# Gate and up chunks: high and low parts of four pairs of plain weight groups made by one instruction per pair

## The reference

```python
def swiglu(x, w_gate, w_up, w_down):
    return (jax.nn.silu(x @ w_gate) * (x @ w_up)) @ w_down

h = h + 0.5 * swiglu(rms_norm(h, ffn1_norm[l]), ffn1_w_gate[l], ffn1_w_up[l], ffn1_w_down[l])
... # mixing block
h = h + 0.5 * swiglu(rms_norm(h, ffn2_norm[l]), ffn2_w_gate[l], ffn2_w_up[l], ffn2_w_down[l])
```

## Time and profile before

| | |
|---|---|
| median of 3 runs | 1835.87 us |
| profiled execution | 1837.03 us |
| its span on the core | 1834.9 us |
| PE busy | 1817.6 us, 99% of the span |
| DVE busy | 1504.9 us, 82% |
| ACT busy | 997.4 us, 54% |
| HBM traffic | 207 GB/s over the span |
| TensorE's granted clock | 0.999 of full speed |

### The profile page before, as it was taken

One profiled execution on the slowest core, in us unless ns is written; L12 is line 12 of the kernel. 1 busy time (PEld: TensorE's weight loads), 2 busy tenths in 40 slices (PEclk: granted clock), 3 DMA queues, 4 the chain that ended last, 5 costly groups with the idle time before them and its releaser, 6 DMA issues.

```text
span 1834.9 us, 29704 instructions
## 1 busy us (share of the span) xinstructions
PE 1817.6 (99%) x10674; PEld 1544.7 (84%) x10674; DVE 1504.9 (82%) x1754; ACT 997.4 (54%) x1181; POOL 11.1 (1%) x23
## 2 busy tenths in 40 slices
PE   8999999999999999999999999999999999999998
PEld 7888888888888888999998878888888888888886
DVE  5888888888998986688966866688888888899996
ACT  7455555555555655754535665545555555555554
POOL 1000000000000000000000000000000000000000
PEclk9999999999999999999999999999999999999999
DMA  7767776777766778565433558577767677676664
GB/s 239 230 212 222 231 221 206 227 218 233 241 199 210 220 227 266 176 185 143 139 111 108 175 171 264 178 229 234 230 220 233 216 226 225 218 237 199 208 216 149
DMA packets 207850, 380.35 MB, mean 207 GB/s; under 512 B 16016, under 2 KB 35728, under 8 KB 207504
## 3 DMA queue, kind: packets, MB, share of 16 engines
q1 hardware_dynamic: 206768, 377.08, 65.3%
q10 hardware_dynamic: 480, 1.97, 0.3%
q0 software_dynamic: 512, 0.06, 0.0%
HBM read 360.19 MB, written 18.87 MB: 207 GB/s over the span
## 4 chain that ended last, share of the span: by engine, by line
PE 92%; DVE 3%; DMA 2%; ACT 1%; issue 1%; SPq 0%; ACTq 0%; DVEq 0%
PE psA L427 30%; PE psB L427 28%; PE psB L1231 6%; PE psT L438 5%; PE psM L438 5%; PE psA L438 5%; PE psA L1231 4%; PE psB L438 2%; PE psM L427 1%; DVE wlo L410 1%; DMA raw<-in_w_in 1%; PE psA L1242 1%; PE psB L650 1%; DMA raw<-in_ffn_w_down 0%; DVE y L1455 0%
## 5 line engine op out<-in xcount | busy, mean ns | idle before, releaser
L401 ACT CAST whi<-raw 128x1024 fp32r<-128x1024 f32 (+1 forms) x648 | 676.6, 1049 | 693.6 <-DVE raw L1455 186.1
L410 DVE TENSOR_TENSOR wlo<-raw,whi 128x1024 fp32r<-128x1024 f32 (+1 forms) x648 | 771.8, 1214 | 205.2 <-ACT whi L401 192.4
L427 PE MATMUL psA<-whi,xh 128*128 128x512 f32 (+1 forms) x576 | 221.8, 385 | 0.5 <-DVE wlo L410 0.5
L427 PE MATMUL psA<-whi,xl 128*128 128x512 f32 (+1 forms) x576 | 221.2, 384 | 0.0
L427 PE MATMUL psA<-wlo,xh 128*128 128x512 f32 (+1 forms) x576 | 221.2, 384 | 0.0
L427 PE MATMUL psB<-whi,xh 128*128 128x512 f32 x544 | 211.7, 389 | 0.0
L427 PE MATMUL psB<-whi,xl 128*128 128x512 f32 x544 | 211.6, 389 | 0.0
L427 PE MATMUL psB<-wlo,xh 128*128 128x512 f32 x544 | 211.6, 389 | 0.0
L427 PEld LDWEIGHTS psA<-whi,xh 128*128 128x128 f32 x576 | 108.4, 188 | 22.0 <-DVE wlo L410 0.7
L427 PEld LDWEIGHTS psA<-whi,xl 128*128 128x128 f32 x576 | 108.4, 188 | 21.3
L427 PEld LDWEIGHTS psA<-wlo,xh 128*128 128x128 f32 x576 | 108.4, 188 | 21.1
(11 more groups left out here) (511 smaller groups left out, 3436.7 us busy)
## 6 DMA issues: line engine op xcount, KB each, us to landing
raw<-in_ffn_w_gate SPq DMA_DIRECT2D x176, 512.0 KB, 4.5
raw<-in_ffn_w_up SPq DMA_DIRECT2D x176, 512.0 KB, 4.6
raw<-in_ffn_w_down SPq DMA_DIRECT2D x176, 512.0 KB, 4.5
raw<-in_w_in SPq DMA_DIRECT2D x80, 512.0 KB, 3.7
raw<-in_w_out SPq DMA_DIRECT2D x32, 512.0 KB, 4.3
quads_dram<-stage SPq DMA_DIRECT2D x88, 128.0 KB, 4.3
stage<-quads_dram SPq DMA_DIRECT2D x22, 512.0 KB, 4.3
x<-in_x SPq DMA_DIRECT2D x4, 512.0 KB, 7.6
```

Source lines behind the costliest of these rows:

```text
L401: nc.scalar.copy(whi[:, slot, :, 0:ncol], raw[:, slot, :, 0:ncol]).then_inc(hi_ready, 1)
L410: nc.vector.tensor_tensor(wlo[:, slot, :, 0:ncol], raw[:, slot, :, 0:ncol], whi[:, slot, :, 0:ncol].bitcast(F32), ALU.subtract).then_inc(l ...
L427: mm = nc.tensor.matmul(ps[:, tb, 0:ncol], lhs[:, k0 + t, tok], rhs[:, slot, t, 0:ncol], start=(first and t == 0 and p == 0 and tb != open ...
```

## The change

In the 20 passes of `chunk(n)`, four pairs of neighbouring plain groups, (0, 1), (2, 3), (6, 7) and (12, 13), are split by one ACT copy and one DVE subtraction of 2048 elements per partition each. The pairs stand in slots that lie side by side (0 and 1, or 2 and 3). The copy waits for both DMAs and for PE to have finished group g - 3, the second one's forerunner in its slot; each instruction counts its semaphore up by 2 at its end. Groups 4, 5, 8 to 11, 14 and 15, the first chunks, the down projections and the mixing block stay as they are, and so do PE's and SP's instructions and their waits.

```diff
--- before.py
+++ after.py
@@ -47,6 +47,7 @@
 CHUNK = ([("gate", j) for j in (0, 1, 4, 5)] + [("unit", 0)] + [("gate", j) for j in (6, 7)] + [("up", 0)] + [("unit", 1)]
          + [("up", j) for j in (1, 4, 5, 6, 7)])
 UNITS = ((7, 7), (7, 8))
+TWO_GROUPS = (0, 2, 6, 12)
 GATE_TOTAL = GATE_UNITS * (FC - 1)
 GATE_STEPS = 5 * (FC - 1)
 PAIR_STEPS = 7
@@ -410,6 +411,22 @@
             nc.vector.tensor_tensor(wlo[:, slot, :, 0:ncol], raw[:, slot, :, 0:ncol],
                                     whi[:, slot, :, 0:ncol].bitcast(F32), ALU.subtract).then_inc(lo_ready, 1)
 
+        def split_hi_two(base, n, per, j):
+            g = base + j
+            two = slice(g % SLOTS, g % SLOTS + 2)
+            wait_raw(nc.scalar, g, n, per)
+            wait_raw(nc.scalar, g + 1, n, per)
+            nc.scalar.wait_ge(group_used, n * per + g - SLOTS + 2)
+            nc.scalar.copy(whi[:, two, :, :], raw[:, two, :, :]).then_inc(hi_ready, 2)
+
+        def split_lo_two(base, n, per, j):
+            g = base + j
+            two = slice(g % SLOTS, g % SLOTS + 2)
+            nc.vector.wait_ge(hi_ready, n * per + g + 2)
+            nc.vector.wait_ge(group_used, n * per + g - SLOTS + 2)
+            nc.vector.tensor_tensor(wlo[:, two, :, :], raw[:, two, :, :],
+                                    whi[:, two, :, :].bitcast(F32), ALU.subtract).then_inc(lo_ready, 2)
+
         def wait_group(base, n, per, j):
 
             nc.tensor.wait_ge(lo_ready, n * per + base + j + 1)
@@ -732,7 +749,10 @@
 
             def chunk(n):
                 for kind, j, g in chunk_items():
-                    split_hi(base, n, PER, g)
+                    if g in TWO_GROUPS:
+                        split_hi_two(base, n, PER, g)
+                    elif g - 1 not in TWO_GROUPS:
+                        split_hi(base, n, PER, g)
                     if kind == "unit":
                         unit = FIRST_UNIT[f] - GATE_UNITS + j
                         nc.scalar.wait_ge(col_step, n * (4 * GATE_UNITS) + (4 * unit + 2))
@@ -958,7 +978,9 @@
                         unit_lo(n, unit)
                         if j == 0:
                             turn_quads(n - 1)
-                    else:
+                    elif g in TWO_GROUPS:
+                        split_lo_two(base, n, PER, g)
+                    elif g - 1 not in TWO_GROUPS:
                         split_lo(base, n, PER, g)
                     if g == 1 and not (isinstance(n, int) and n == 1):
                         turned_lo(n - 2)
```

## The result

The changed kernel takes 1904.52 us, median of 4 runs (1902.49 to 1906.25), against 1837.38 for the kernel before beside it (4 runs, 1835.83 to 1840.04): a ratio of 1.0361, 95% interval 1.0346 to 1.0377, some 67 us slower. The profiled execution's span went from 1834.9 to 1903.6 us.

What follows compares the result with a forecast made beforehand. PE was taken as the bound, without gaps; stalls of 1.5, 0.1 and 1.3 us make 2.86 a pass, by 20 passes 57.2, on 1837.03 giving 1894.2, less 1.2 for the median: 1893 us, own range 1872 to 1914.

Steps and rivals of the forecast that it cites:

- PE has no gap to lose and can only be made late: In a pass PE runs 186 matmuls 0.2267 us apart without gap; savings on DVE or ACT can't make it earlier.
- The wide instructions: ACT's copy and DVE's subtraction of 2048 elements per pair: 1.92 and 2.29 us forecast, bounded by 0.2 us for both together.
- First and second step: Pair (2, 3) starts DVE's gating 1.93 us later; nothing gives it back up to unit 0, just met with 0.1 us lost.
- Third step: At pair (6, 7): its subtraction ends at 412.29, PE wants group 6 at 410.83, a stall of 1.5 us.
- Fourth step: Load of group 10 issued 3.0 us later, usable after 4.32; unit 1's sums slip, PE loses 0.1 us more at group 9.
- Fifth step: Pair (12, 13): load 13 usable 4.32 us after issue, PE starts group 12 at 429.34 instead of 426.48, 1.3 us more.
- The handing over: Time from the end of a pair's subtraction to PE's start, 0.05 us in the stall before group 6.
- The pair (0, 1) is met: At the start of the next pass, 4.4 - 1.6 - 1.9 leaves 0.9 us before PE's need, so no stall.
- No change: Rival: group 6's margin of 1.5 us and the others hold, 1836 us; chance 0.05.
- faster: Rival: DVE's instruction stream paces PE in the passes, so 80 pairs give back 6.4 us, 1830 us; chance 0.03.
- only the first stall: Rival: only the stall at group 6 shows and pair (12, 13) is met, 1.5 us by 20, 1867 us; chance 0.10.
- a third stall: Rival: a stall also at pair (0, 1), its 0.9 us used up, 1 us by 20 more, 1913 us; chance 0.12.

## Why the prediction was right, and where its size was off

1893 us was forecast, 1904.5 measured, inside the range; by the difference to the kernel before beside it, 57 us forecast and 67 measured.

- *PE has no gap to lose and can only be made late.* Shown: every kernel with gaps is slower by about their sum, and the one with the fewest (two pairs) is not faster.
- *The wide instructions* (1.92 and 2.29 us). 1.91 and 2.28. The prediction's words that the two lines have one slope don't hold; each has its own, 432 ns per 512 elements for the copy and 534 for the subtraction, and these gave the two figures.
- *First and second step* (gating and what follows 1.93 us late, unit 0 just met). Measured 2.01 for the gating. The gap of 0.1 us came before group 4 and not at the low part of the sums, and with the cost of starting again it is 0.27 in the mean, more than "just met".
- *Third step* (1.5 us before group 6). Group 6 starts 1.55 us late. Without the pair (2, 3) this gap is gone, and without the transpose ahead of it 0.11 are left.
- *Fourth step* (load 10 at 17.20 us into the pass, used 4.32 us later). 17.27, and 4.23; the means are 17.31 and 4.28. The latency was borrowed from load 13, "alone" in the queue, while load 10 itself had taken 4.85 in the pass read and 4.39 in the mean. That it fitted is in part luck: load 13 was not alone either, the load back was issued 2.6 us ahead of it in that pass. DVE's idle before the sums was to stay at 2.7 us; the chain itself gives 3.3, and 3.22 were measured.
- *Fifth step* (load 13 issued at 25.54 us into the pass, used 4.32 us later). 25.52, but 4.66 in the pass shown. **This is the mis-sized term.** Both latencies of the sum were one row of one pass. The mean over 18 passes was at hand, 4.54 for load 13 in the kernel before; in the changed one it is 4.72, in place of 4.32. That is 0.4 us a pass, 8 us. Half of it was to be read beforehand (4.54 less 4.32). Of the other 0.18, 0.12 lie between landing and copy: a pair's copy starts 0.21 us after load 13 has landed, the single one started 0.09 after; the load itself lands after 4.51 in place of 4.45.
- *The handing over.* Each of PE's stalls costs more than the wait: after 412.28 the next matmul starts 0.34 us on, not 0.23. The last such start of a pass isn't taken up by the chain, 0.11 us a pass.
- Together, by the means of 18 passes: load 10 issued 0.11 us later than forecast and used 0.04 sooner, load 13 used 0.40 later, 0.05 more from the copy of the pair (12, 13) to PE's start, 0.11 for that start and 0.04 in small lengthenings behind it. That is 0.67 on 2.86, 3.53 for a later pass. The first pass of each block loses only 2.1, since group 6 had 2.2 and 2.4 us of margin there and not 1.5. The forecast took all 20 for alike.
- *The pair (0, 1) is met.* Right: in the pass shown its subtraction ends 0.8 us before PE's need (0.9 forecast; 420.23 + 2.29 against 423.31), and no gap stands before group 0.
- *Rivals.* No change, faster, and "only the first stall" fall by the traces; a third stall didn't come.
- The rule of the Trainium skill (VectorE: DVE Perf Modes, on the TRN2 errata), that one large tile pays the fixed latency once, held in the rows: the wide subtraction occupies DVE for 2.21 us (380.03 to 382.24), two single ones in a row for 2.28. DVE was busy 9.9 us less in all (1504.9 to 1495.0; 6.4 forecast). It bought no time.

Open is why loads land as they do: the runs show that the load back costs load 13 0.6 us where it is issued in front, not what in the queues does it.

## What to carry to other kernels

Where the busiest engine has no gap, a wider instruction on the way to it saved nothing here and made the first half of its output late; compare that delay with the margin between ready and needed at each place, and follow who issues the next load on it. The losses don't belong to a pair by itself (15 us for the pair (2, 3) alone, 3 for (0, 1) and (6, 7), 33 and 37 for three, 67 for four) but to the chain that runs through several. Read a latency that the sum counts as a mean over all passes, and look for the wait that stands right behind the one that you shorten.

## What was not expected of the hardware

- After a stall PE's first matmul of 512 columns holds up the next for 0.34 us and not 0.23 (394.94 to 395.28 above). So a stall has a fixed cost of 0.11 us beside its wait, and a wait of 0.16 us in the mean before group 4 becomes 0.27 with it. In the five traces counted (the changed kernel, those without the pair (2, 3), with single instructions, with the transpose moved and with the load back moved), every wait of more than 0.13 us was followed by 0.33 to 0.34.
- A 512 KB load issued 2.1 us behind another 512 KB load was usable after 4.72 us in the mean, and with that one issued 0.5 us behind it after 4.10.
- Load 10 was usable after 4.28 us in the mean where the four 128 KB stores began 0.45 us behind it, and after 3.90 where they began 1.11 behind. The kernels without the pair (2, 3) show the same, 4.19 and 3.88. What else changed in the queues is not separated.
